# Expert results queued behind dense weights, a gated turn around a key group, one joint norm factor: seven edits to a two-block transformer kernel

## What is computed

```python
for l in range(DEPTH):                        # DEPTH = 2
    xn = modulate(rms_norm(h, g_norm_mix[l]), sh1, sc1)
    p = xn @ w_in[l]
    y_a = diff_post(diff_attention_latent(qa, ka, va, ka_c, va_c, lam), da_subln_g[l], lam_init)
    y_b = spatial_gating(p[..., OFF_ZB:OFF_GATE], ...)
    y_c = neighbourhood_attention(...)
    h = h + gt1 * merge_branches(p[..., OFF_GATE:], y_a, y_b, y_c, w_branch[l], w_out[l])
    xn2 = modulate(rms_norm(h, g_norm_ffn[l]), sh2, sc2)
    h = h + gt2 * hier_moe(xn2, ...)          # 32 experts, a row goes to some of them
h = rms_norm(h, g_final)                      # first block ends
# second block
z = rmsnorm(h, pre_mix_g) @ w_in_2            # GLA, short conv, dilated attention from z
h = h + rmsnorm(merged @ w_mix_out, post_mix_g)
h = h + rmsnorm((gelu(conv(rmsnorm(h, pre_ffn_g) @ w_ff_gate)) * up) @ w_ff_down, post_ffn_g)
```

## Time and profile before

| what | us |
|---|---|
| median of 3 runs | 2712.97 |
| lowest, highest run | 2710.84, 2713.23 |
| span of the profiled execution | 2710.1 |
| that execution's own time | 2711.93 |
| PE busy | 2493.7 (92% of the span) |
| DVE, ACT, POOL busy | 772.5, 460.6, 170.9 |

### The profile page before, as it was taken

How to read it: one execution, slowest core, us unless ns; L and a number is a source line. 1 busy time by engine, 2 the same in 40 slices (tenths; PEclk the granted TensorE clock), 3 DMA queues, 4 the chain that set the end, 5 groups by cost and what they waited for, 6 DMA issues and landing times.

```text
span 2710.1 us, 30408 instructions
## 1 busy us (share of the span) xinstructions
PE 2493.7 (92%) x12208; PEld 1524.1 (56%) x12208; DVE 772.5 (29%) x1640; ACT 460.6 (17%) x1039; POOL 170.9 (6%) x195
## 2 busy tenths in 40 slices
PE   8999999999987778799999989777879999999998
PEld 3444554445554444445577655444445688887873
DVE  2694444115311111154343321000002323212210
ACT  2121223101100000022132110000002122102320
POOL 0000000000111111000000011111100000000000
PEclk9999999999999999999999999999999999999999
DMA  8464010424999999964424599999985332344331
GB/s 327 166 241 183 31 63 32 172 108 185 415 425 425 426 426 425 401 240 189 183 94 159 224 425 422 424 426 426 424 372 225 144 125 94 140 155 153 146 142 56
DMA packets 63047, 666.41 MB, mean 246 GB/s; under 512 B 13059, under 2 KB 13347, under 8 KB 24401
## 3 DMA queue, kind: packets, MB, share of 16 engines
q1 hardware_dynamic: 48672, 636.78, 57.4%
q0 software_dynamic: 13392, 24.82, 2.5%
q10 hardware_dynamic: 864, 3.15, 0.3%
HBM read 664.28 MB, written 21.02 MB: 253 GB/s over the span
## 4 chain that ended last, share of the span: by engine, by line
PE 74%; DMA 21%; DVE 2%; issue 2%; ACT 2%; POOL 0%; SPq 0%; DVEq 0%; ACTq 0%; POOLq 0%
DMA ring<-in_w_moe 11%; PE act_bank L733 7%; PE act_bank L722 7%; PE act_bank L852 6%; PE score_bank L1150 5%; PE act_bank L1290 5%; PE vec_bank L868 4%; PE vec_bank L1162 4%; PE vec_bank L1033 4%; PE score_bank L852 3%; PE vec_bank L852 3%; PE act_bank L1527 3%; PE vec_bank L1527 3%; PE vec_bank L1545 3%; DMA xT<-in_w_moe 3%; DMA heads<-in_w_moe 3%
## 5 line engine op out<-in xcount | busy, mean ns | idle before, releaser
L733 PE MATMUL act_bank<-xT,ring 128*128 128x512 f32 (+1 forms) x512 | 193.4, 539 | 0.0
L722 PE MATMUL act_bank<-ring,xT 128*128 128x512 f32 x416 | 183.5, 597 | 2.1 <-DVE xT L2137 1.6
L2575 DVE TENSOR_TENSOR heads<-work,vec_bank 128x256 f32<-128x256 f32 x64 | 27.0, 421 | 505.3 <-PE vec_bank L1150 505.3
L852 PE MATMUL act_bank<-xT,ring 128*128 128x256 f32 (+1 forms) x576 | 157.7, 427 | 1.9 <-issue 1.5
L733 PEld LDWEIGHTS act_bank<-xT,ring 128*128 128x128 f32 x512 | 97.1, 190 | 95.0 <-issue 91.8
L1150 PE MATMUL vec_bank<-ring,branches 128*64 128x256 f32 x1024 | 120.6, 389 | 27.7 <-DMA ring<-in_w_moe 27.7
L1150 PE MATMUL score_bank<-ring,branches 128*64 128x256 f32 x1024 | 122.5, 393 | 23.9 <-issue 12.5
L1162 PE MATMUL vec_bank<-ring,heads 128*64 128x512 f32 x512 | 116.9, 598 | 26.9 <-DMA ring<-in_w_moe 17.4
L852 PEld LDWEIGHTS act_bank<-xT,ring 128*128 128x128 f32 x576 | 109.2, 190 | 44.1 <-issue 32.0
L722 PEld LDWEIGHTS act_bank<-ring,xT 128*128 128x128 f32 x416 | 78.5, 191 | 97.7 <-issue 97.7
L1290 PE MATMUL act_bank<-xT,ring 128*128 128x256 f32 x576 | 126.6, 380 | 0.6 <-ACT work L1943 0.6
(11 more groups left out here) (412 smaller groups left out, 3349.7 us busy)
## 6 DMA issues: line engine op xcount, KB each, us to landing
ring<-in_w_moe SPq DMA_DIRECT2D x96, 2048.0 KB
ring<-in_w_in SPq DMA_DIRECT2D x29, 2048.0 KB
ring<-in_w_merge SPq DMA_DIRECT2D x27, 2048.0 KB
branches<-in_w_moe SPq DMA_DIRECT2D x24, 2048.0 KB
heads<-in_w_moe SPq DMA_DIRECT2D x24, 2048.0 KB
ring<-in_w_ada SPq DMA_DIRECT2D x23, 2048.0 KB
xT<-in_w_moe SPq DMA_DIRECT2D x22, 2048.0 KB
values<-in_w_moe SPq DMA_DIRECT2D x22, 2048.0 KB
```

Of the source, the lines that this page charges most:

```text
L722: mm = pe.matmul(b.t[:, :], xT[:, k, tile * P:(tile + 1) * P], w[:, k * COLS:(k + 1) * COLS], start=(k == 0), stop=(k == KD - 1))
L733: mm = pe.matmul(b.t[:, 0:n], w[:, k * COLS + f * P:k * COLS + (f + 1) * P], xT[:, k, 0:n], start=(k == 0), stop=(k == KD - 1))
L852: mm = pe.matmul(g.t[:, 0:n], merge_tile(l, i, MERGE_TILES * d + k), xs[:, k, 0:n], start=(k == 0), stop=(k == KD - 1))
```

## The change

1. **Gated rows** (layer 0): PE turns two tiles, then does the first group of 8 matmuls of KC, then turns the other two. ACT follows the same order. Layer 1 has two tiles and stays.
2. **Neighbourhood** (both layers): `exps(1)` stands behind the evacuations of item 0.
3. **Results**: tile 0 goes to `branches[2048:4096]`, tiles 1 and 2 to `heads[2048:4096]` and `heads[4096:6144]`. In layer 1 chunk U is issued first, then the result of tile 0, then V and VA, then the results of tiles 1, 2, 3. Tile 0 waits for the scatters and for the last reader of slot 4, only tile 1 for `last_gate`. In block 2 each of the two results stands behind its chunk instead of ahead.
4. **Entry of block 2**: DVE multiplies halves of `h` by `final_g` into `x2first`, ACT takes the squares of these too, both roots come from one power of POOL over two columns, and DVE scales `x2first` once. `h = h * r * final_g` is done after the turned columns of the tile.
5. **Mixed norm**: the turn goes tile by tile (`turn_mixed`), into S[tile] and V[tile]; tile 0 is turned between the first and the second half of tile 1's product. 12 instead of 20 steps of `keep_going` follow.
6. ACT writes four of tile 0's turned columns behind the squares of tile 1's first half, and
7. DVE writes the other four between the two halves' gains of tile 1.

The core of the diff:

```diff
-    y_tile = [heads[:, 2048:4096], heads[:, 4096:6144], branches[:, 2048:4096], heads[:, 0:2048]]
+    y_tile = [branches[:, 2048:4096], heads[:, 2048:4096], heads[:, 4096:6144], heads[:, 0:2048]]
...
-            for tile in range(nt):
-                pe.wait_ge(*mark["yb", l, tile])
-                turn_rows(yb, tile, S)
-            columns_chunk(("in", l, "KC"), NT * P)
+            turn_yb(range(2))
+            columns_chunk(("in", l, "KC"), NT * P, lambda: turn_yb(range(2, nt)))
...
+        def turn_mixed(tile):
+
+            pe.wait_ge(xhat_done.sem, NT * DEPTH + 2 + tile + 1)
+            for q, b in enumerate((S[tile], V[tile])):
                 pe.wait_ge(b.free, b.fills)
+                for j in range(4):
+                    f = 4 * q + j
+                    mm = pe.transpose(b.t[:, j * P:(j + 1) * P], x2hat[:, tile, f * P:(f + 1) * P], ident)
...
-        for tile in range(2):
-            for c in range(OUT_CHUNKS):
-                out_product(2, tile, c, 0, KD)
-        pe.wait_ge(V[0].free, V[0].fills)
-        keep_going(20, V[0])
-        norm2_columns()
+        for c in range(OUT_CHUNKS):
+            out_product(2, 0, c, 0, KD)
+        out_product(2, 1, 0, 0, KD)
+        turn_mixed(0)
+        out_product(2, 1, 1, 0, KD)
+        pe.wait_ge(A[1].free, A[1].fills)
+        keep_going(12, A[1])
+        turn_mixed(1)
...
-                if i + 1 < len(pairs):
+                if 0 < i < len(pairs) - 1:
                     exps(i + 1)
                 half_tanh_between(l, 1, 2 * i, parts)
                 kt = n_keys(tile) // P
                 for m in range(2):
                     evacuate(A[m], mixT[:, m, 0:kt, :], n=kt * P, shape=kt)
+                if i == 0:
+                    exps(1)
...
             for c in range(OUT_CHUNKS):
                 half_squares(V[2 + c].t[:, :], tile, c, 0.5, *mark["summed", 2, tile, c])
+                if (tile, c) == (1, 0):
+                    turned_mixed(0)
...
-                STT(out=h[:, tile, :], in0=h[:, tile, :], scalar=r, in1=final_g, op0=ALU.mult, op1=ALU.mult)\
-                    .then_inc(final_done.sem, final_done.up())
-                root_mean(tile, tile + 1)
-                TS(x2first[:, tile, :], h[:, tile, :], r, None, ALU.mult).then_inc(xhat_done.sem, xhat_done.up())
+                for c in range(2):
+                    half = slice(c * COLS, (c + 1) * COLS)
+                    dve.wait_ge(*mark["added", DEPTH - 1, tile, c])
+                    TT(x2first[:, tile, half], h[:, tile, half], final_g[:, half], ALU.mult)\
+                        .then_inc(final_done.sem, final_done.up())
...
+                step(TS(r2, r, EPS, None, ALU.mult))
...
+                power(STT(out=r2, in0=sq_b[:, 2 + tile:3 + tile], scalar=1.0 / D, in1=r2, op0=ALU.mult, op1=ALU.add))
+                TS(x2first[:, tile, :], x2first[:, tile, :], r2, None, ALU.mult).then_inc(xhat_done.sem, xhat_done.up())
...
+                step(STT(out=h[:, tile, :], in0=h[:, tile, :], scalar=r, in1=final_g, op0=ALU.mult, op1=ALU.mult))
...
-                add_normed(tile, V[2:], mix_g, 0.5)
+                add_normed(tile, V[2:], mix_g, 0.5, (lambda: turned_mixed(0)) if tile else None)
...
+                sp.wait_ge(*last_read(max(c for c, s in AT.items() if c[:2] == ("expert", l) and s[0] == NSLOT)))
+            if tile == 1:
                 sp.wait_ge(*mark["last_gate", l])
...
-        result_ahead = {("in", 1, "U"): (0, 0), ("in", 1, "V"): (0, 1), ("in", 1, "VA"): (0, 2),
-                        ("in2", 2, IN2_ORDER[0]): (1, 0), ("in2", 2, IN2_ORDER[1]): (1, 1)}
+        results_behind = {("in", 1, "U"): ((0, 0),), ("in", 1, "VA"): tuple((0, tile) for tile in range(1, NT)),
+                          ("in2", 2, IN2_ORDER[0]): ((1, 0),), ("in2", 2, IN2_ORDER[1]): ((1, 1),)}
```

More of the change, by code:

```diff
@@ L551, in h_done_mix @@
         return sum(2 * tiles(k) for k in range(l + 1))
-    o2r_power = sum(NT + 3 * tiles(l) for l in range(DEPTH)) + 2 * 2 + 1
+    o2r_power = sum(NT + 3 * tiles(l) for l in range(DEPTH)) + 2 + 1
     def at_bank(b):
@@ L1675, in turned @@
         def turned(br, nt, scale=None):
-            for tile in range(nt):
+            for tile in nt:
                 dst = ysT[:, br, :, tile * P:(tile + 1) * P]
@@ L1771, in differential @@
             act.wait_ge(mod_done.sem, l + 1)
[L1772 removed]
+            turned(0, range(tiles(l)), scale=sub_g[:, l:l + 1])
             n = streams(l) * ADA_KINDS * KD
@@ L1935, in second_in, with turned_mixed @@
             evacuate(A[1], dv[:, 1, 0:COLS])
-        def norm2_columns(gain):
-            for f in range(KD):
-                evacuate(A[f % 2], x2T[:, f, :], ACT.Identity, n=SEQ, scale=col(gain)[:, f:f + 1])
+        def turned_mixed(tile):
+            b = S[tile]
+            act.wait_ge(*mark["mixed_T", tile, 0])
+            for f in range(4):
+                ins = nc.scalar.activation(x2T[:, f, tile * P:(tile + 1) * P], b.t[:, f * P:(f + 1) * P], ACT.Copy,
+                                           scale=col("pre_ffn_g")[:, f:f + 1])
+            ins.then_inc(b.free, 1)
         def linear_attention_in():
@@ L2924, in square_sum, with add_normed @@
             dve.wait_ge(pow_out.sem, pow_in.n)
-        def add_normed(tile, banks, gain, scale):
+        def add_normed(tile, banks, gain, scale, between=None):
             def weighed(c):
+                if c == 1 and between is not None:
+                    between()
                 STT(out=y2[:, tile, c * 512:(c + 1) * 512], in0=banks[c].t[:, :], scalar=scale,
@@ L2940, in mixed_norm, with turned_mixed @@
         def mixed_norm():
+            def turned_mixed(tile):
+                b = V[tile]
+                dve.wait_ge(b.full, b.reads + 1)
+                for j in range(4):
+                    f = 4 + j
+                    ins = TS(x2T[:, f, tile * P:(tile + 1) * P], b.t[:, j * P:(j + 1) * P], col("pre_ffn_g")[:, f:f + 1], None,
+                             ALU.mult)
+                ins.then_inc(b.free, b.read())
             for tile in range(2):
-                add_normed(tile, V[2:], mix_g, 0.5)
+                add_normed(tile, V[2:], mix_g, 0.5, (lambda: turned_mixed(0)) if tile else None)
                 square_sum(tile, 2 + tile, lambda c: None)
@@ L3132, in _ @@
         for tile in range(2):
-            for _ in range(2):
-                power(rstd[:, tile:tile + 1], rstd[:, tile:tile + 1])
+            both = rstd.rearrange("p (a b) -> p b a", b=2)[:, tile, :]
+            power(both, both)
             if tile == 0:
```

59 lines of the change are left out of this document (35 added, 24 removed).

## The result

The changed kernel takes **2719.8 us** (median of 11 runs, 2717.5 to 2721.4); the kernel before, run beside it, 2712.8 (11 runs, 2710.4 to 2717.4). The ratio is 1.0027, 95% interval 1.0019 to 1.0035: slower by 7.1 us, by the ratio's interval 5 to 9.5. The forecast was 2719.7 and +6.7. The span of the profiled execution went from 2710.1 to 2717.8, +7.7.

What follows compares the result with a forecast made beforehand. Weight stream sets the pace in expert stages, PE elsewhere (74% of the chain of waits). Terms -2.1 - 2.4 + 9.8 + 4.0 - 0.5 - 2.1 = +6.7 on 2713.0 gave 2719.7 us, range 2712.0 to 2726.0.

Steps and rivals of the forecast that it cites:

- The landing: Entries of layer 1 and block 2: first result lands behind its chunk, in issue order, +4.9 us each, together +9.8.
- The clock: Both entries: about 7 us of PE idle brings the low clock, 2.0 us each, together +4.0.
- The bound of 3.4: Both entries: one clock fall costs at most twice the 1.69 us of one profile row.
- The mixed norm's term: Before the feed-forward: idles of 2.0 and 1.3 us can bring the low clock, up to 1.8 us lost.
- Gated rows and neighbourhood: PE's waits at the gated rows (-2.1 us) and in both layers' neighbourhood (-2.4 us) go.
- these gains pass the experts whole: Layer 0: earlier gains aren't swallowed by the experts, since PE's own progress releases their weight stream.
- one sign missed: Layer 1's entry: the first L2679, DVE's start on the result, was to come near 1150.1 us.
- Second holder in layer 1: Layer 1's entry: tile 1's result, then cond_rows, delay tile 1's columns, leaving about +5.1 us.
- the slower rival: Layer 1: cond_rows takes 14 to 17 us, not 10.6, costing 2 to 5 us more, 2722 to 2725; chance 0.08.
- Joint factor: Entry of block 2: tile 0 gains -0.3 us, tile 1 -0.2, sum -0.5; bounds -0.5 and +1.3.
- Mixed norm: Before the feed-forward: first matmul 3.0 us earlier; with possible clock loss -2.1 taken, bounds -3.0 and -1.2.

Runs made afterwards that it cites:

- the run through POOL's queue: Tile 0's result issued by POOL in POOL's queue, same waits, both entries, against the changed kernel: 2709.2 us beside 2712.6, ratio 0.9985.
- the filled run: 14 more filler steps in PE's wait before tile 0's last product, both entries, against the changed kernel: 2714.2 us beside 2712.6, ratio 1.0006.
- part 3 alone: Only the results' new places, waits and issue order, put into the kernel before: 2727.2 us beside 2712.6, ratio 1.0053.

## Why the prediction was right, step by step

**The landing, right.** The term was +4.9 at each entry, measured +5.0. It came from one pair of rows (7.4 us for 3 MB) read as "in order of issue". Tile 1's result was foreseen at 1165.6 and landed at 1163.9, 1165.7 without the 1.8 that lay ahead. The run with the early issue ahead of U shows that the reading holds where issue and landing are 17 us apart, and the run through POOL's queue that it is a matter of SP's queue alone.

**The clock, right in sum, wrong in part.** +2.0 at each entry was taken, +2.6 and +1.8 came. The bound of 3.4 held. But the term was laid on entries of the kernel before that cost no clock, as its one trace has them, and that was luck at layer 1: behind waits of 2.53 to 2.69 the clock fell in seven of nine places (five of seven at layer 1, both in block 2), behind those of 2.00 to 2.04 in block 2 in none of five. By these counts a longer wait at layer 1 adds less, in most executions, than the difference of these two traces. The mixed norm's term (0 to 1.8, taken 0.9) measured 1.4 in the changed kernel and 0 to 3.1 in eight traces, so its upper bound was too low: I had priced it by the 1.69 of one row, and the stretch at the low level can be longer than that row's.

**Gated rows and neighbourhood, right in the trace:** -2.1 and -2.6 where -2.1 and -2.4 were summed. The statement that these gains pass the experts whole was too plain. In the changed kernel's trace 2.3 us of it were gone by the end of layer 0's experts. About 1.3 is the clock at the first products, the rest is not more than the stage varies by. Hence one sign missed: DVE's first row of layer 1 came at 1151.74, not near 1150.1.

**Second holder in layer 1, right in kind, small in size.** I had put it at +5.1; the filled run shows it at +6.1 (PE's wait there, with the shift of what lies ahead taken off), against the +7.65 that layer 1's entry had in all. The missing 1.0 is mostly in the landing of `cond_rows`: I let it move by 8.5, though the result that it waits for was to move by 9.8, and gave no reason; it moved by 9.4, with the 1.8 added. So the 10.6 us of `cond_rows` had 1.6 us of room and the slower rival didn't come, since the load took 10.2.

**Joint factor, right in kind, small in size:** -0.5 was summed as its best; it is -0.8 where the clock is full, and -0.3 of it shows in the changed kernel, since PE comes late to the first turn there with the old factor too (part 3 alone shows no wait at it). **Mixed norm, right:** -2.8 before the clock, for -3.0; the waits were 1.65 and 1.61, foreseen 2.0 and 1.3.

**Why the total lies so close.** +8.0 from the edits where +6.7 was forecast; the median moved by 7.1. That it fits to the tenth is chance. The steps that no edit made are each as large as 2 us in a profiled execution, and the kernel before alone has medians 1.9 us apart in its batches.

## What to carry to other kernels

Where one queue is full, as here, a transfer lands by its place in it, not by the time of its issue: count the MB ahead of it (2.46 us each here), and put what is waited for ahead of what is not. Price a wait of the matmul engine by its length plus the slow stretch behind it, and fill it with useless matmuls that end just before the release: here 6.6 us went with it, though no release came earlier. One trace has one draw of the clock at each wait; look at a second execution before you take a short wait as free. Before moving a transfer to another queue in a stage that bandwidth bounds, name what it pushes back.

## What the runs showed of the hardware that I had not expected

- The granted clock fell behind waits of 1.00 us (5.41 us for 16 matmuls in two traces, 3.72 in twelve) and of 1.61 us (in six of eight), in some executions and not in others. The Trainium skill ("TensorE: Matmul & The Clock Gate", section "HAM oscillation — how this bites in real kernels") describes such a loss behind waits for transfers, paid in the work that follows; the rows here agree for the waits of 7 us, in all four places that have one, and show it behind far shorter ones, now and then.
- It goes with the spread of the times: 2704.9 to 2710.6 without fillers in the small waits, 2698.4 to 2701.6 with them. Of 17 runs of the kernel before in one batch the fastest (2707.2) had a mean granted clock of 0.995 and the slowest (2719.4) 0.989.
- 1 MB issued by POOL took 8.8 to 12.4 us while SP's queue was full (six transfers), against 17.4 to 20.5 in that queue (the first results of two kernels), and the weight pieces that the first one passed in layer 1 came 2.4 us later.
